# Moving a projection into the sample attention, an earlier low part in the recurrence, and a new bank and group order in the expert stage

## What is computed

```
h    = rms_norm(x) * (1 + scale1) + shift1
proj = h @ w_in            # [q|k|v of 12 heads | f | i | hq | hg | gate A | gate B]
A    = dilated window attention: prompt on itself, sample on its caches and itself
B    = HGRN2 recurrence over (f, i, hq), gated with silu(hg)
x    = x + gate1 * ((sigmoid(gA)*(A@w_att) + sigmoid(gB)*(B@w_hg)) @ w_out)
h2   = rms_norm(x) * (1 + scale2) + shift2
y    = for each token: 8 heads x 16 of 16384 experts:
       sum of gate * gelu(h2 . u[e]) * v[e]      # done densely over all experts here
x    = x + gate2 * y ; final rms_norm
```

## Time and profile before

| what | us |
|---|---|
| median of 3 runs (lowest to highest) | 5075.16 (5073.82 to 5082.77) |
| the profiled execution's own time | 5069.28 |
| its span | 5067.6 |
| PE busy in the span | 4449.0 (88%) |
| DVE busy | 2393.8 (47%) |
| ACT busy | 1124.5 (22%) |
| POOL busy | 980.8 (19%) |
| mean granted clock of PE | 0.94 |

### The profile page before, as it was taken

One profiled execution on the slowest core, in us unless ns is written; L12 is line 12 of the kernel. 1 busy time (PEld: TensorE's weight loads), 2 busy tenths in 40 slices (PEclk: granted clock), 3 DMA queues, 4 the chain that ended last, 5 costly groups with the idle time before them and its releaser, 6 DMA issues. The chain is left out here.

```text
span 5067.6 us, 67239 instructions
## 1 busy us (share of the span) xinstructions
PE 4449.0 (88%) x26722; PEld 2305.7 (45%) x26722; DVE 2393.8 (47%) x4394; ACT 1124.5 (22%) x1398; POOL 980.8 (19%) x551
## 2 busy tenths in 40 slices
PE   4998865698674989999999969999999999999993
PEld 3674431355433534555555534444444444444441
DVE  4232114566434205888888735555554332332324
ACT  4232112233322112333333310001001111111113
POOL 0000000222001000000000035555554222222220
PEclk8999877899796999999999989999999999999997
DMA  5332344321453125789966676677675444444432
GB/s 171 101 106 85 104 103 167 95 83 63 144 174 108 67 72 153 250 238 280 281 194 199 203 183 143 143 151 147 144 148 116 98 96 92 100 100 88 100 68 81
DMA packets 1025827, 688.92 MB, mean 136 GB/s; under 512 B 847026, under 2 KB 922890, under 8 KB 1017355
## 3 DMA queue, kind: packets, MB, share of 16 engines
q1 hardware_dynamic: 1013716, 591.63, 46.0%
q10 hardware_dynamic: 4896, 71.31, 3.4%
q0 software_dynamic: 6976, 22.55, 1.2%
HBM read 442.99 MB, written 205.97 MB: 128 GB/s over the span
## 5 line engine op out<-in xcount | busy, mean ns | idle before, releaser
L2640 PE MATMUL ex_psy<-ex_vhi,ex_wboth 128*128 128x512 f16 x4352 | 1322.3, 379 | 41.8 <-issue 41.8
L2640 PE MATMUL ex_psy<-ex_vlo,ex_wboth 128*128 128x512 f16 x2304 | 874.0, 379 | 0.0
L2330 POOL TENSOR_SCALAR ex_v<-ex_v 128x1024 f32<-128x1024 f32 x128 | 396.7, 3099 | 2322.7 <-DMA ex_v<-in_peer_v_dram 2322.3
L2599 PE MATMUL ex_psa<-h_hi,ex_uth 128*128 128x512 f16 (+1 forms) x3072 | 641.2, 318 | 73.7 <-ACT ex_wa L2355 50.1
L2640 PEld LDWEIGHTS ex_psy<-ex_vhi,ex_wboth 128*128 128x128 f16 x4352 | 426.0, 98 | 556.6 <-issue 43.8
L2599 PE MATMUL ex_psa<-h_lo,ex_uth 128*128 128x512 f16 (+1 forms) x3072 | 641.8, 318 | 0.0
L2599 PE MATMUL ex_psa<-h_hi,ex_utl 128*128 128x512 f16 (+1 forms) x3072 | 641.6, 318 | 0.0
L2581 DVE TENSOR_TENSOR ex_acc<-ex_acc,ex_psy 128x512 f32<-128x512 f32 x558 | 372.4, 683 | 477.3 <-PE ex_psy L2640 476.9
L2570 DVE SCALAR_TENSOR_TENSOR ex_wa<-ex_wa,ex_gate 128x1088 f32<-128x1088 f32 x128 | 201.3, 1572 | 532.2 <-ACT ex_wa L2355 503.9
L2355 ACT ACTIVATE ex_wa<-ex_psa 128x1088 f32<-128x1088 f32 x128 | 137.9, 1077 | 1206.6 <-PE ex_psa L2599 1206.5
L2599 PEld LDWEIGHTS ex_psa<-h_hi,ex_uth 128*128 128x128 f16 x3072 | 234.6, 98 | 320.2 <-issue 69.6
(11 more groups left out here) (365 smaller groups left out, 5678.8 us busy)
## 6 DMA issues: line engine op xcount, KB each, us to landing
gate_all<-rt_stage ACTq DMA_DIRECT2D x34, 2048.0 KB, 6.7
ex_gate<-gate_all SPq DMA_DIRECT2D x128, 544.0 KB
ex_u<-in_peer_u_dram SPq DMA_DIRECT2D x128, 512.0 KB, 5.2
ex_v<-in_peer_v_dram SPq DMA_DIRECT2D x128, 512.0 KB, 8.1
act_all<-ex_wa SPq DMA_DIRECT2D x80, 544.0 KB, 3.5
ex_wa<-act_all SPq DMA_DIRECT2D x80, 544.0 KB, 3.8
ad_w<-in_ada_w_dram SPq DMA_DIRECT2D x8, 2048.0 KB, 8.0
pa_w<-in_w_in_dram SPq DMA_DIRECT2D x10, 1024.0 KB, 7.9
```

What stands on the lines that cost most here:

```text
L2330: nc.gpsimd.tensor_scalar(v[s][:, :], v[s][:, :], SPLIT, None, ALU.mult).then_inc(v_sc, 1)
L2599: mm = nc.tensor.matmul(ps_a[:, c:e], x[s][:, k, :], h[:, k, c:e], start=(k == 0 and j == 0), stop=(k == KD - 1 and j == len(mms) - 1))
L2640: mm = nc.tensor.matmul(ps_y[n % YB][:, :], w, v_[:, a * 512:(a + 1) * 512], start=(j == 0), stop=(j == len(mms) - 1))
```

## The change

The stage "pt" is gone. Its 8 chunks are made inside the sample attention: each of the 24 quarters gets one `fill`, a third of a chunk (512, 512 or 64 token columns, 24 matmuls each), between the transposes and the scores of its keys. Two PSUM banks alternate for the fills; the banks for this come from putting `ps_o` and `ps_n` into one bank, for which PE now waits for `picked` before the first scores of a pass. Weights come in 8 loads of 128 columns and results leave in 8 stores, all on SP's queue. The two halves of the batch, a hardware loop before, are written out.

In the recurrence DVE does `low(n + 1)` ahead of its wait for `msum` (L1666) and no more at the end of the tile.

In the expert stage the products of a block go span by span (512, 512, 64 token columns) and not triple by triple. `ps_a` has five banks: the two wide spans alternate between two banks each, the narrow one has one. Gelu is three instructions, one for each span. The order of groups changes: the first group behind the 80 blocks is an unmade one (blocks 80 to 83), made in `half(0, None, 0)`; then come the 20 kept groups, then the 11 other unmade ones.

```diff
@@ mixer
-        project_features(pr, "pt", h_hi, h_lo, w_v, C_ZQ, 2 * HW, t["proj_t"], 0, 2 * P)
+        pr.clear_semaphores()
+        attention_sample(pr, h_hi, h_lo, w_v)
...
@@ attention_sample, SP
+            for c in range(2):
+                load_weights(c)
+            for i in range(2):
                 for g in range(3):
+                    n = i * 3 + g
+                    if n >= 2:
+                        load_weights(n)
+                    if n >= 3:
+                        store(n - 3)
                     sp.wait_ge(pv_done, i * 3 + g + 1)
...
+            for c in range(6, CHUNKS):
+                store(c - 3)
+                load_weights(c)
+            for c in range(CHUNKS - 3, CHUNKS):
+                store(c)
...
@@ attention_sample, PE
+            def fill(q):
+                c, u, s = q // UNITS, q % UNITS, q // UNITS % 2
+                a, e = u * 512, min(u * 512 + 512, TOK)
+                if u == 0:
+                    pe.wait_ge(w_lo_done, c + 1)
+                pe.wait_ge(emptied, q + 1)
+                for k in range(KD):
+                    for j, (x, h) in enumerate(((zw_hi, h_hi), (zw_hi, h_lo), (zw_lo, h_hi))):
+                        mm = nc.tensor.matmul(ps_z[q % 2][:, 0:e - a], x[s][:, k, :], h[:, k, a:e],
+                                              start=(k == 0 and j == 0), stop=(k == KD - 1 and j == 2))
+                mm.then_inc(filled, 1)
...
                         mm.then_inc(ktr, 1)
+                        fill(q)
+                        if b == 0:
+                            pe.wait_ge(picked, n + 1)
                         pe.wait_ge(kt_done, q + 2)
...
-                    pe.wait_ge(picked, n + 1)
@@ attention_sample, ACT
                         nc.scalar.copy(k_t[b % 2][:, :, 0:w], ps_k[:, :, 0:w]).then_inc(kt_done, 1)
+                        if q:
+                            empty(q - 1)
+                        if q % UNITS == 1 and 2 <= q // UNITS + 1 < CHUNKS:
+                            high(q // UNITS + 1)
...
@@ attention_sample, DVE
+            for c in range(2):
+                low(c)
...
+                    if n in (1, 3, 4):
+                        low({1: 2, 3: 5, 4: 6}[n])
                     dve.wait_ge(scored, n * 4 + 6)
...
+                    if n in (1, 2, 4):
+                        low({1: 3, 2: 4, 4: 7}[n])
                     dve.wait_ge(p_turned, n + 1)
...
@@ recurrence, DVE
+                if n + 1 < PT:
+                    low(n + 1)
                 dve.wait_ge(msum, n + 1)
...
                 dve.sem_inc(tile_done, 1)
-                if n + 1 < PT:
-                    low(n + 1)
...
@@ experts
+    SPANS = ((0, 512), (512, SEQ), (SEQ, TOK))
+    bank_of = lambda c, s: (s * 2 + c, s * 2 + c, 4)[c] * 512
...
                 half(0, None, 0)
-                half(1, 0, 1)
+                half(1, 0, 1, True)
                 with eng.Fori(1, FIRST // 2) as i:
                     half(i * 2, i * 2 - 1, 0, True)
                     half(i * 2 + 1, i * 2, 1, True)
-                with eng.Fori(FIRST // 2, NGR // 2 - 1) as i:
+                half(FIRST, FIRST - 1, 0, True)
+                half(FIRST + 1, FIRST, 1)
+                with eng.Fori(FIRST // 2 + 1, NGR // 2 - 1) as i:
...
+                if isinstance(g1, int) and g1 == 0:
+                    return AHEAD + b
+                return g1 * EB + b - EB if kept else g1 * EB + b
...
@@ experts, SP
-                for s in range(2):
-                    sp.wait_ge(wa_stored[s], AHEAD // 2 * 16)
                 sp.wait_ge(routed, PT + 1)
...
@@ experts, ACT
                 def gelu(eb, s):
-                    act.wait_ge(acted, eb + 3)
-                    nc.scalar.activation(wa[s][:, :], ps_a[:, 0:TOK], ACT.Gelu_apprx_tanh, scale=1.0 / SPLIT).then_inc(gelu_done, 1)
+                    for c, (a, e) in enumerate(SPANS):
+                        act.wait_ge(acted, eb * 3 + c + 7)
+                        nc.scalar.activation(wa[s][:, a:e], ps_a[:, bank_of(c, s):bank_of(c, s) + e - a],
+                                             ACT.Gelu_apprx_tanh, scale=1.0 / SPLIT).then_inc(gelu_done, 1)
...
@@ experts, PE
+                    for c in spans:
+                        a, e = SPANS[c]
+                        at = bank_of(c, s)
+                        pe.wait_ge(gelu_done, eb * 3 + (c + 1 if c < 2 else 6))
+                        for k in range(KD):
+                            for j, (x, h) in enumerate(((ut_h, h_hi), (ut_h, h_lo), (ut_l, h_hi))):
+                                mm = nc.tensor.matmul(ps_a[:, at:at + e - a], x[s][:, k, :], h[:, k, a:e],
+                                                      start=(k == 0 and j == 0), stop=(k == KD - 1 and j == 2))
                         mm.then_inc(acted, 1)
...
-                        products(eb, eb % 2, range(0, 4))
+                        products(eb, eb % 2, (0,))
                         scatter((n - 1) * PER_TILE + 2 * j - 1)
-                        products(eb, eb % 2, range(4, 8))
+                        products(eb, eb % 2, (1, 2))
                         scatter((n - 1) * PER_TILE + 2 * j)
```

More of the change, by code:

```diff
@@ L1218, in attention_sample @@
     kv_in = [pr.sem(f"as_in{g}") for g in range(3)]
+    w_in, z_stored = ([pr.sem(f"as_{n}{s}") for s in range(2)] for n in ("win", "zstored"))
+    w_hi_done, w_lo_done, filled, emptied = (pr.sem(f"as_{n}") for n in ("whi", "wlo", "filled", "emptied"))
+    CHUNKS, UNITS = 2 * HW // P, 3
     NKB = (1, 4, 4)
@@ L1267, in _ @@
                 pe.wait_ge(new_t, g + 1)
+            def fill(q):
[9 more added lines that the diff above has]
+                mm.then_inc(filled, 1)
             pe.sem_inc(pv_done, 3)
             pe.sem_inc(scored, 2)
-            with pe.Fori(0, 2) as i:
+            for i in range(2):
                 for g in range(3):
@@ L1291, in _ @@
                             lhs = qbd[g][:, hp, b].rearrange("p h t -> p (h t)")
-                            mm = nc.tensor.matmul(ps_n[rows, 0:NS], lhs, new_tt[:, 1, g, hp, :], start=(hp == 0), stop=(hp == 1))
+                            mm = nc.tensor.matmul(ps_n[rows, :], lhs, new_tt[:, 1, g, hp, :], start=(hp == 0), stop=(hp == 1))
                         mm.then_inc(scored, 1)
@@ L1309, in _, with high, empty @@
         def _(act):
+            def high(c):
+                act.wait_ge(w_in[c % 2], c // 2 * 16 + 16)
+                if c >= 2:
+                    act.wait_ge(filled, (c - 1) * UNITS)
+                nc.scalar.activation(zw_hi[c % 2][:, :, :], zw[c % 2][:, :, :], ACT.Copy, scale=SPLIT).then_inc(w_hi_done, 1)
+            def empty(q):
+                c, u = q // UNITS, q % UNITS
+                a, e = u * 512, min(u * 512 + 512, TOK)
+                act.wait_ge(filled, q + 1)
+                if u == 0 and c >= 2:
+                    act.wait_ge(z_stored[c % 2], c // 2 * 16)
+                nc.scalar.activation(z[c % 2][:, a:e], ps_z[q % 2][:, 0:e - a], ACT.Copy, scale=1.0 / SPLIT).then_inc(emptied, 1)
             act.sem_inc(kt_done, 1)
-            with act.Fori(0, 2) as i:
+            act.sem_inc(emptied, 2)
+            for c in range(2):
+                high(c)
+            for i in range(2):
                 for g in range(3):
@@ L1337, in _ @@
             dve.sem_inc(picked, 1)
-            with dve.Fori(0, 2) as i:
+            for c in range(2):
+                low(c)
+            for i in range(2):
                 for g in range(3):
@@ L2587, in _, with products @@
                 pe.wait_ge(ready, 2)
[L2588 to L2592 removed]
+                pe.sem_inc(acted, 6)
+                def products(eb, s, spans):
+                    if spans[0] == 0:
                         pe.wait_ge(ut_in[s], (eb - s) * 16 + 32)
[L2594 to L2601 removed]
+                    for c in spans:
[6 more added lines that the diff above has]
+                                                      start=(k == 0 and j == 0), stop=(k == KD - 1 and j == 2))
                         mm.then_inc(acted, 1)
@@ L2654, in half @@
                     for b in range(EB):
-                        if g1 is not None and not is_kept(g1, kept):
-                            eb = g1 * EB + b
-                            products(eb, b % 2, range(KD))
+                        if g1 is not None and not kept:
+                            eb = block_at(g1, b, kept)
+                            products(eb, b % 2, (0, 1, 2))
                         if g2 is not None and b == 0:
```

88 lines of the change are left out of this document (48 added, 40 removed).

## The result

The changed kernel takes 4891.59 us (median of 4 runs, 4889.74 to 4893.37) against 5074.49 us for the kernel before on the same chip (4 runs): the ratio is 0.9636, 95% interval 0.9620 to 0.9651. The forecast was 4899.0 us. Timed again later beside other kernels it took 4888.61 us (5 runs, 4887.46 to 4893.34). The profiled execution took 4889.74 us, 179.5 less than that of before; its span is 4888.1 us.

The account below looks back on a forecast made before the run. PE was taken to bound the experts, so only its waits could be won there. Terms -43 - 36 - 61 - 35 = -175 us took 5069.3 to 4894, plus 5.9 for the median: about 4899 us, range 4868 to 4942.

Parts of the forecast that it names:

- 1. Projection into the sample attention: Sample attention: fills replace the 107.6 us projection stage and hide PE's waits for key copies; -43 us, bounds -62 to -22.
- the clock, taken at 4 us net: Sample attention: fills keep PE's clock high longer, but exponential rests stay and the first fill starts low; 4 us net gain.
- Rival C: Sample attention keeps its low clock and PE waits for caches or weights: -22 us there, 4920 us in all; 15 in 100.
- 2. Low part in the recurrence: Recurrence: low part in DVE's idle time removes 24.5 us of PE waits and 7 x 1.7 us of clock falls; -36 us.
- the late `kh` of the lower bound: Recurrence: DVE's next step, `kh`, turns up late, so that only -12 us is won.
- rival D: Recurrence gives only part of its 24.5 us, as `kh` or the clock stays: -15 us, 4920 us in all; 8 in 100.
- 3. Two sets of banks: The 80 expert blocks: PE's 48.8 us of gelu waits and 12.7 us of drains go; -61 us, bounds -40 to -65.
- Rival A: Expert blocks: narrow products standing alone show their weight loads, 98 ns instead of 29; 212 us more, 5111 us; 3 in 100.
- Rival B: DVE binds the 80 expert blocks, 13.31 us of work against a 12.9 us period; half the gain lost, 4930 us; 12 in 100.
- 4. An unmade group first: Experts, ahead of the first unit: 44.2 us of products from four blocks fill PE's 41.84 us rest; -35 us, bounds -41 to -14.
- not hidden: Experts, behind the last block before the first unit: the chain gelu, DVE, ACT, DVE stays as a PE rest of 7.5 us.
- Rival E: Transition to the first unit stalls on gates and transposing DMAs: only -14 us there, 4920 us in all; 13 in 100.

## Why the prediction was right

The total was 7 us too high, and each of the four parts came within some 7 us of its term. About 4 of the 7 us are the step from the profiled execution to the median, taken at 5.9 us and 1.9 us here.

**1. Projection into the sample attention: -43 predicted, about -50 measured.** The 107.6 us went, and the copy waits hid nearly as said (21.3 - 1.6 = 19.7 us; all but about a microsecond was foreseen). The mis-sized term is the clock, taken at 4 us net because "the rests for the exponential stay". At the prediction's prices PE's work would be 119.75 + 88.5 = 208.3 us; it is 199.1 us, 9 us less, and 6 us less in the slowest of the eight traces. The rests for the exponential did stay (15.6 us in 6 places), so the reason was right and the size was not. The sum also left out a rest of PE in the kernel before, which is gone now:

```profile
PE as_ps_k L1282 <- DVE as_qbd L1345: 2.9, 1, 2.9
```

The stage of "about 255 us" takes 250, and 252 to 252.5 in four of the eight traces. That hiding counts is shown by moving the fill, which takes back 29 of the 50 us; 7 to 9 of these are PE's own work. Rival C is out: no wait for weights, and the rests ahead of key transposes are what they were (10.5 and 6.1 us in the list of waits, 10.1 and 6.2 before).

**2. Low part in the recurrence: -36 predicted, -34 measured.** The wait and the clock came as the sum has them: 24.5 us, and 9.9 instead of 11.9. A tile takes 35.4 us between two `kt` (from 40.7; 35.8 were foreseen). The late `kh` of the lower bound shows in one wait of 1.8 us, which the kernel before had too, with 1.7 us; rival D is out.

**3. Two sets of banks: -61 predicted, -64 measured, and the reason is one of two.** The price (48.8 us of waits and 0.16 us of drain each) was right, and so was the period, 12.9 us. The cause given for it, that "the wide spans have a second bank", is enough but not needed: with second banks and late gelus the time is the same, and so it is with one bank and early gelus. Two thirds of the gain need neither, but only that gelu is three instructions, which the prediction treated as an added cost for ACT to hide. The sum came out since the changed kernel has more than it needs; that the reason was incomplete could not show in the total. Rival A is out: the last narrow span of a block still runs its products 0.029 us apart, as the timeline of the changed kernel has it (23 steps between these rows).

```profile
2260.76 0.19 PE L2597 MATMUL ex_psa<-h_hi,ex_uth 128*128 128x64 f16 x1
...
2261.43 0.19 PE L2597 MATMUL ex_psa<-h_hi,ex_utl 128*128 128x64 f16 x1
```

The rule that spoke against the change, in the Trainium skill's "TensorE: Matmul & The Clock Gate", Part 3, that a weight load overlaps only matmuls of another row group, does not describe these rows; each of these products has a weight load of its own in the trace and all use the whole array. (The prediction's "other weights than the one before" holds for two products of three: the second of a triple loads the same weights again.) The same page's "Step-by-step: what each phase is for" also lets a load go ahead when it fills a background weight buffer, and with that the trace agrees, though it does not show the buffer. Rival B is out as well, by a hair: DVE has 12.75 us of work in a block of 12.89, and PE waited 1.6 us for it in all.

**4. An unmade group first: -35 predicted, -33 measured.** The arithmetic of 44.2 us moved into the rest holds, PE being busy for 55.45 of 55.50 us. (The terms add up to -34.3, which was rounded up.) The step that was off is what is "not hidden": 7.5 us were put down to gelu, DVE, ACT, DVE behind the last block. That chain took 4.9 us, from the end of the last product at 2869.94 to 2874.83, and the 8.9 us were set by POOL and the DMA of the last values. The prediction had seen v behind other work on SP's queue, and feared gates, not values. That 7.5 us lies within the 7.1 to 9.7 us of the traces is luck, as what set the rest was another chain. Rival E (stalls between the blocks) is out.

Undone one by one, parts 2, 3 and 4 cost some 33, 71 and 34 us; with the 50 of part 1, read from the trace alone, that makes 188, against 183 for the whole. The blocks 80 to 83 account for the 5 us: undoing part 3 makes them wait too (4 x 1.5 us), which they do only since part 4 made them stand in a row. Otherwise the parts hardly touch each other. Part 1 as a whole was not undone on the chip.

## What to carry to other kernels

When an engine waits for a reader to free a buffer, ask first how large a piece the reader frees at a time; cutting its instruction at the buffers' borders gave 50 us here without a second buffer, as other work covered the shorter wait. Independent work that is moved into a latency-bound stage should be cut to the length of that stage's rests and dealt to all of them: the same matmuls gave 50 us at one place per quarter and, with 46.5 us more, 96 in small pieces. When a rest has been filled, read again what ends what is left of it; it need not be the chain that ended it before.

## What was not expected of the hardware

- **The clock fell with short rests.** In the sample attention rests of 0.5 to 1.1 us ahead of each fill, some 20 us in all, came with a mean granted clock of 0.86 and not 0.89, and with nearly all rests gone it was 0.96. The matmuls are the same 1140; PE's work on them went from 208.6 to 181.9 us. The 20 us of rests made the stage 27 to 30 us longer, some 1.4 times their length.
- **A DMA share above 1.** The profile shows 1.05 and 1.18 in some windows, so this figure can't be read as a share of a limit; in the first of these windows PE was busy throughout.
- **DVE at 99% of the period** (12.75 of 12.89 us) did not hold PE up; in all 80 blocks PE waited 1.6 us for it.
